# Two attentions: the spread of 1/sum by a transpose of reciprocals that ACT has written 64 times side by side

## The reference, cut to what matters

```python
# layer 0, latent tokens
s_nb = jnp.einsum('bqhd,biwhd->bhqiw', q_r, k_b) * scale + bias
s_cx = jnp.einsum('bqhd,bshd->bhqs', q_r, kc) * scale
p = jax.nn.softmax(jnp.concatenate([s_nb, s_cx], axis=-1), axis=-1)
o = einsum('bhqn,bnhd->bqhd', p[..., :n_nb], v_b) + einsum('bhqs,bshd->bqhd', p[..., n_nb:], vc)
# layer 1
s = jnp.einsum('bqhgd,bshd->bhgqs', q_b, k_all) * scale
p = jax.nn.softmax(s, axis=-1)
o = jnp.einsum('bhgqs,bshd->bqhgd', p, v_all)
```

## Time and profile before

| | |
|---|---|
| runs (3), us | 1558.33, 1562.14, 1561.76, median 1561.76 |
| the profiled execution, us | 1563.42, its span 1562.1 |
| PE busy | 1534.3 us, 98% of the span |
| PE weight loads | 1293.1 us, 83% |
| DVE busy | 928.9 us, 59% |
| ACT busy | 693.3 us, 44% |
| POOL busy | 64.7 us, 4% |
| DMA | 251 MB, mean 161 GB/s |
| attention 0, attention 1 | about 179 to 262 us and 755 to 809 us of the span |

### The profile page before, as it was taken

The page is one execution under the profiler, slowest core; times in us unless marked ns, Lnnn a source line. Parts: engine busy times, 40 slices in busy tenths (PEclk is TensorE's granted clock), DMA queues, the critical chain, the costliest instruction groups (busy, mean ns, idle before and its releaser), DMA issues.

```text
span 1562.1 us, 22713 instructions
## 1 busy us (share of the span) xinstructions
PE 1534.3 (98%) x9647; PEld 1293.1 (83%) x9647; DVE 928.9 (59%) x1208; ACT 693.3 (44%) x950; POOL 64.7 (4%) x92
## 2 busy tenths in 40 slices
PE   6999999999999999999999999999999999999998
PEld 4777766768888888879778888899999999999987
DVE  5422586463434333466866676668788856678863
ACT  4311475242312222235764545545555546555543
POOL 2010030000000000000000000034000000000000
PEclk9999999999999999999999999999999999999999
DMA  9664432654432332463134555665555554555552
GB/s 359 226 208 163 141 44 77 231 189 135 163 106 81 108 108 68 139 231 130 55 136 135 181 181 174 218 198 179 172 190 189 173 191 149 185 187 182 189 189 81
DMA packets 244165, 251.45 MB, mean 161 GB/s; under 512 B 17134, under 2 KB 237649, under 8 KB 244065
## 3 DMA queue, kind: packets, MB, share of 16 engines
q1 hardware_dynamic: 242528, 247.48, 48.8%
q0 software_dynamic: 928, 1.87, 0.3%
q10 hardware_dynamic: 608, 0.66, 0.1%
HBM read 248.94 MB, written 1.05 MB: 160 GB/s over the span
## 4 chain that ended last, share of the span: by engine, by line
PE 83%; DVE 7%; ACT 4%; POOL 2%; issue 2%; SPq 1%; DMA 1%; DVEq 0%; ACTq 0%; POOLq 0%
PE psum L366 80%; DVE wl L352 3%; ACT wh L345 3%; PE psum L954 2%; DMA raw<-in_na_w_qkv 1%; POOL ptmp L1860 1%; SPq L292 1%; DVE sums L1010 0%; DVE scr L1754 0%; ACT scr L1721 0%; DVE scr L1752 0%; DVE scr L1746 0%; POOL ptmp L1859 0%; DVE scr L542 0%; POOL scr L1867 0%
## 5 line engine op out<-in xcount | busy, mean ns | idle before, releaser
L352 DVE TENSOR_TENSOR wl<-raw,wh 128x2048 fp32r<-128x2048 f32 (+1 forms) x185 | 418.2, 2262 | 267.9 <-ACT wh L345 267.6
L345 ACT ACTIVATE wh<-raw 128x2048 fp32r<-128x2048 f32 (+1 forms) x185 | 348.0, 1883 | 380.2 <-PE psum L366 370.2
L366 PE MATMUL psum<-x,wh 128*128 128x256 f32 (+1 forms) x1792 | 446.0, 329 | 1.3 <-DVE x L552 0.8
L366 PE MATMUL psum<-x,wl 128*128 128x256 f32 x1248 | 351.6, 282 | 0.0
L366 PEld LDWEIGHTS psum<-x,wh 128*128 128x128 f32 x1792 | 302.3, 190 | 34.1 <-issue 3.1
L366 PE MATMUL psum<-xh,wh 128*128 128x512 f32 (+1 forms) x688 | 259.9, 378 | 3.1 <-DVE xl L705 2.4
L366 PE MATMUL psum<-xh,wl 128*128 128x512 f32 (+1 forms) x688 | 255.9, 372 | 0.0
L366 PE MATMUL psum<-xl,wh 128*128 128x512 f32 (+1 forms) x688 | 255.8, 372 | 0.0
L366 PEld LDWEIGHTS psum<-x,wl 128*128 128x128 f32 x1248 | 237.4, 190 | 0.1
L366 PEld LDWEIGHTS psum<-xh,wh 128*128 128x128 f32 x688 | 130.8, 190 | 35.3 <-issue 5.3
L366 PEld LDWEIGHTS psum<-xh,wl 128*128 128x128 f32 x688 | 130.7, 190 | 22.4
(11 more groups left out here) (277 smaller groups left out, 1957.0 us busy)
## 6 DMA issues: line engine op xcount, KB each, us to landing
raw<-in_ffn_w_in SPq DMA_DIRECT2D x44, 1024.0 KB, 5.0
pre<-in_ada_w SPq DMA_DIRECT2D x25, 1024.0 KB, 10.6
raw<-in_ada_w SPq DMA_DIRECT2D x23, 1024.0 KB, 5.5
raw<-in_w_ffn_gate SPq DMA_DIRECT2D x22, 1024.0 KB, 5.1
raw<-in_w_ffn_up SPq DMA_DIRECT2D x22, 1024.0 KB, 5.1
raw<-in_w_ffn_down SPq DMA_DIRECT2D x19, 1024.0 KB, 4.9
raw<-in_ffn_w_out SPq DMA_DIRECT2D x16, 1024.0 KB, 5.2
raw<-in_na_w_qkv SPq DMA_DIRECT2D x12, 1024.0 KB, 5.2
```

The lines of the kernel that those rows point to most:

```text
L345: act.e.activation(wh[:, c % NSPL, 0:z], raw[:, p % NRAW, 0:z], ACT.Copy).then_inc(W.hi, 1)
L352: dve.e.tensor_tensor(wl[:, c % NSPL, 0:z], raw[:, p % NRAW, 0:z], wh[:, c % NSPL, 0:z].bitcast(F32), ALU.subtract).then_inc(W.lo, 1)
L366: return pe.e.matmul(o, l, r, start=start, stop=stop, skip_group_check=shared)
```

## The change

A new tile `wide` (two groups, two query tiles, two heads, 64; 2 KiB a partition) takes the reciprocals, each written 64 times by ACT. For each group PE turns it with two transposes of 128x128, one for each query tile, both heads side by side. The reciprocals on DVE move ahead of the wait for the transposes and of DVE's copy. On ACT the wait for the reciprocals and the wide write stand after the exponentials and ahead of the copy L990. PE's wait for the reciprocals goes, since the wait for ACT's copy holds for the wide write too; that wait and DVE's stand ahead of the spread now. The tile's places in the arena and the tables' first column are the rest.

```diff
     def __init__(...)
+        self.wide = wide
...
+        wide0 = at(54, "wide0", [P, 2, 2, 2, 64])
+        wide1 = at(38, "wide1", [P, 2, 2, 2, 64])
...
             def values_part(g, first, last):
 
-                at_, u, nc_ = A_.groups[g]
+                u, nc_ = A_.groups[g]
                 o = bank[6 + g % 2]
                 if first:
-                    pe.wait_ge(S.recip, b_.recip + u + 1)
                     if g == 0 and value:
                         value()
                     if g >= 2:
                         pe.wait_ge(S.scaled, b_.scaled + g - 1)
-                    for x in range(2):
-                        for h in range(2):
-                            mm(o[64 * h:64 * h + 64, T + x * P:T + x * P + P], A_.sums[:, 2, at_ + x, h:h + 1].to_broadcast([P, 64]),
-                               ident, True, True)
                     pe.wait_ge(S.copied_a, b_.copied_a + u + 1)
                     pe.wait_ge(S.copied_d, b_.copied_d + u + 1)
+                    for x in range(2):
+                        pe.e.transpose(o[:, T + x * P:T + x * P + P], A_.wide[:, g % 2, x, :, :].rearrange("p h d -> p (h d)"), ident)
...
                 j = i - 2
                 if 0 <= j < n:
-                    g = A_.units[j][0]
-                    act.wait_ge(S.turned, b_.turned + j + 1)
+                    g, parts, x, at_ = A_.units[j]
                     if g >= 2:
                         act.wait_ge(S.pv, b_.pv + g - 1)
+                    act.wait_ge(S.recip, b_.recip + j + 1)
+                    act.e.activation(A_.wide[:, g % 2, x:x + parts, :, :],
+                                     A_.sums[:, 2, at_:at_ + parts, :].unsqueeze(3).to_broadcast([P, parts, 2, 64]), ACT.Copy)
+                    act.wait_ge(S.turned, b_.turned + j + 1)
                     to, o = turned(A_, j, 0)
                     act.e.activation(to, o, ACT.Copy).then_inc(S.copied_a, 1)
...
                 if 0 <= j < n:
                     g, parts, _, at_ = A_.units[j]
+                    dve.wait_ge(S.exp, b_.exp + 2 * j + 2)
+                    dve.e.reciprocal(A_.sums[:, 2, at_:at_ + parts, :], A_.sums[:, 1, at_:at_ + parts, :]).then_inc(S.recip, 1)
                     dve.wait_ge(S.turned, b_.turned + j + 1)
                     if g >= 2:
                         dve.wait_ge(S.pv, b_.pv + g - 1)
                     to, o = turned(A_, j, 1)
                     dve.e.tensor_copy(to, o).then_inc(S.copied_d, 1)
-                    dve.wait_ge(S.exp, b_.exp + 2 * j + 2)
-                    dve.e.reciprocal(A_.sums[:, 2, at_:at_ + parts, :], A_.sums[:, 1, at_:at_ + parts, :]).then_inc(S.recip, 1)
```

More of the change, by code:

```diff
@@ L83, with __init__ @@
 class Attention:
-    def __init__(self, S, base, units, groups, steps, pt, rb, sums, scale, rms, hi, lo):
+    def __init__(self, S, base, units, groups, steps, pt, rb, wide, sums, scale, rms, hi, lo):
         self.S, self.base, self.units, self.groups, self.steps = S, base, units, groups, steps
-        self.pt, self.rb, self.sums, self.scale, self.rms, self.hi, self.lo = pt, rb, sums, scale, rms, hi, lo
+        self.pt, self.rb, self.wide, self.sums, self.scale, self.rms, self.hi, self.lo = pt, rb, wide, sums, scale, rms, hi, lo
         self.n = len(units)
@@ L141, in program @@
         cz = rstd[:, :].rearrange("p (k n) -> p k n", k=KT)
-        pt0, rb0 = at(70, "pt0", [P, 2, 2, 4, T]), at(86, "rb0", [P, 2, T])
+        pt0, rb0, wide0 = at(70, "pt0", [P, 2, 2, 4, T]), at(86, "rb0", [P, 2, T]), at(54, "wide0", [P, 2, 2, 2, 64])
         xh1, xl1 = at(0, "xh1", [P, KT, TT], F32R), at(16, "xl1", [P, KT, TT], F32R)
@@ L151, in program @@
         xh4, xl4 = at(48, "xh4", [P, KT, T], F32R), at(56, "xl4", [P, KT, T], F32R)
-        pt1 = at(64, "pt1", [P, 2, 2, 4, T])
+        pt1, wide1 = at(64, "pt1", [P, 2, 2, 4, T]), at(38, "wide1", [P, 2, 2, 2, 64])
         acc2 = at(74, "acc2", [P, TT])
@@ L1049, in program @@
         units0 = [(2 * p + (kind > 0), 2 if kind == 0 else 1, max(kind - 1, 0), 4 * p + (0, 2, 3)[kind]) for p in range(8) for kind in range(3)]
-        groups0_ = [(4 * p + 2 * lat, 3 * p + 2 * lat, 4 if lat else 2) for p in range(8) for lat in range(2)]
+        groups0_ = [(3 * p + 2 * lat, 4 if lat else 2) for p in range(8) for lat in range(2)]
         steps0 = Steps(*zip(*[((3 * p + 5, 3 * p + 6, True, 3 * p + 6) if lat else (3 * p + 4, 3 * p + 4, False, 3 * p + 4))
@@ L1055, in side0 @@
             return slice(0, T) if g % 2 else slice(T, TT)
-        C0 = Attention(A0, A0._make([0] * len(A0)), units0, groups0_, steps0, pt0, rb0, sums0, lambda j, h: 1.0, None,
+        C0 = Attention(A0, A0._make([0] * len(A0)), units0, groups0_, steps0, pt0, rb0, wide0, sums0, lambda j, h: 1.0, None,
                        lambda g: xh1[:, g // 2, side0(g)], lambda g: xl1[:, g // 2, side0(g)])
@@ L1507, in program @@
         steps1 = Steps([2 * g + 4 for g in range(8)], [2 * g + 5 for g in range(8)], [False] * 8, [2 * g + 5 for g in range(8)])
-        C1 = Attention(A1, base1, [(j // 2, 1, j % 2, j) for j in range(16)], [(2 * g, 2 * g + 1, 4) for g in range(8)], steps1, pt1, rb1,
+        C1 = Attention(A1, base1, [(j // 2, 1, j % 2, j) for j in range(16)], [(2 * g + 1, 4) for g in range(8)], steps1, pt1, rb1, wide1,
                        sums0, lambda j, h: rms1(j)[:, h:h + 1], rms1, lambda g: xh4[:, g, :], lambda g: xl4[:, g, :])
```

## The result

| | before | after |
|---|---|---|
| first set of runs, median, us | 1560.39 (13 runs) | 1563.52 (13 runs) |
| ratio, 95% interval | | 1.0024 (1.0016 to 1.0033) |
| the same two kernels again, us | 1559.76 (17) | 1564.80 (6) |
| ratio, 95% interval | | 1.0033 (1.0022 to 1.0045) |
| profiled execution, us; span | 1563.42; 1562.1 | 1562.95; 1561.6 |

What follows compares the result with a forecast made beforehand. PE bounded both attentions before; after the change a round of ACT and DVE would. Attention 0 +4.9 and attention 1 +1.5 sum to +6.4 us: 1569.8 against the profiled 1563.42, 1568.2 as a median; range 1560.5 to 1573.5.

Steps and rivals of the forecast that it cites:

- The write's price: ACT's wide write of the repeated reciprocals: 0.20 us for 128 elements a partition, 0.31 us for 256.
- a dearer price: The Trainium skill's ACTIVATE price for ACT's wide writes, 0.41 and 0.51 us; it would have made the total +9.9 us.
- rb and handover to L1034: First unit with bias, attention 0: ACT writes rb in 0.41 us, then 0.10 us until DVE starts L1034.
- pair, attention 0: One ACT and DVE round over three units takes 10.9 us, against 9.70 for PE and 10.16 before.
- lead used up by the tenth score: Start of attention 0: the first pairs still have a lead to use up, +0.25 us by the tenth score.
- four full periods: Steady part of attention 0: four pairs, each 0.74 us longer than before, together +3.0 us.
- last pair and draining, attention 0: End of attention 0: the last pair's own period and about 1 us of late transposes, together +1.7 us.
- A handover costs 0.10 us: Between ACT and DVE in each unit: one engine starts 0.10 us after the other ends, read from two places.
- the walk: PE, ACT and DVE queues carried forward through both attentions, each instruction starting when queue and waits allow; total +6.4 us.
- The forecast's lower end, +3.7: Both attentions: wide writes of 0.15 us give +4.7, handovers of 0.05 us from DVE to ACT take another 1 off.
- rival E: TensorE's clock falls to half throughout both attentions, 67 us more, 1628 us in all; chance 0.02.
- A: The forecast itself: the round of ACT and DVE bounds both attentions, 1568.2 us, own range 1565.5 to 1571.7; chance 0.80.

## Why the prediction was right or wrong

**Right, step by step.** That PE alone bounded both stages; that the change takes some 5.5 us from it (with the reciprocals early, pairs of 9.73 and 6.08, forecast 9.70 and 6.07); that this does not arrive, because ACT's wait for a reciprocal that stands behind the maxima joins ACT and DVE into one round; which waits would show and about how long (0.61 to 1.23 us before the wide writes for 0.7 to 1.4, 0.55 to 0.82 on DVE for 0.7 to 0.9, 0.22 and 0.28 on PE for 0.3 to 0.4); that the round outlasts PE's pair. The write's price was right too: 0.21 us from start to start for 128 elements (228.94 to 229.15) and 0.32 for 256 (236.23 to 236.55), forecast 0.20 and 0.31. The prediction set the rows against a dearer price, 0.41 and 0.51 us, and that price was not the one for this write: the Trainium skill (ScalarE: Activation LUTs, Rules for kernel authors) gives it for an ACTIVATE whose bias is a pointer operand, and the wide write has none. For one with immediate scale and bias the same page of the Trainium skill (What ACT_TABLE_LOAD costs) has 186 ns and 0.833 ns an element, less some 93 ns where one overlaps the next. That makes an estimate of 0.29 and 0.40 us of duration, 0.20 and 0.31 from start to start, and the trace agrees: 0.31 and 0.42 of duration, 0.21 and 0.32 of step. What counts in the queue is the step.

**Wrong: the size,** 6.4 us forecast, 3.7 and 5.1 measured, 4.8 in the profile. The terms that were mis-sized:

| term | forecast | measured |
|---|---|---|
| reciprocal and handover to the write | 0.26 | 0.25, 0.19 (232.41 to 232.60) and 0.26 |
| rb and handover to L1034 | 0.41 + 0.10 | 0.41 (233.29 to 233.70) |
| unit without bias | 3.02 | 2.99 (227.49 to 230.48) |
| first unit with bias | 3.74 | 3.56 (230.48 to 234.04) |
| second unit with bias | 4.15 | 4.18 (234.04 to 238.22) |
| pair, attention 0 | 10.90 | 10.73 |
| maxima with L1015, attention 1 | 1.50 | 1.46 (788.63 to 790.09) |
| pair, attention 1 | 6.58 | 6.35 |
| lead used up by the tenth score | +0.25 | -0.1 |
| four full periods | +3.0 | +2.2 |
| last pair and draining, attention 0 | +1.7 | +1.7 |
| attention 0 | +4.9 | +3.8 |
| attention 1 | +1.5 | +1.0 |

The step that failed is "A handover costs 0.10 us", put on every link of the round alike. It was read from two rows, L1015 to ACT and xh to L1038, and it holds for xh to L1038 (230.04 to 230.14) and, at 0.09, for two reciprocals of three. From the other reciprocal to the write it is 0.04 (232.56 to 232.60), and from rb to L1034 0.03 (233.67 to 233.70); rb itself took 0.38 where 0.41 was put in. These two links, 0.19 for 0.26 and 0.41 for 0.51, make the whole difference in the pair of attention 0, 0.17 us, of which 0.03 is rb's own length. It is 1.6% of the round, but the forecast is made of a difference: 10.90 - 10.16 is 0.74, 10.73 - 10.16 is 0.57. In attention 1 the excess over PE's old pair was 0.05 instead of 0.28 us. The same two links account for 0.15 of these 0.23 us, and the maxima with L1015, 1.46 for 1.50 in each of two units, for the rest:

```profile
788.63 1.28 DVE L1010 TENSOR_REDUCE sums<-psum 128x1 f32<-128x512 f32 x2
...
790.09 0.16 DVE L1020 RECIPROCAL sums<-sums 128x2 f32<-128x2 f32 x1
...
790.28 0.31 ACT L986 ACTIVATE wide<-sums 128x128 f32<-128x128 f32 x1 [0.51 <-DVE sums L1020]
```

In attention 0 the links explain the four full periods (+2.2 for +3.0). Two parts of the gap stay open. The lead at the start of attention 0 was worth 0.35 us more than the walk gave it, and no run takes that apart. And the attentions together are 4.8 us longer in the profile, while the runs of the first set say 3.7 (2.5 to 5.1): what the rest of the program gives back in the median, no experiment separates.

The forecast's lower end, +3.7, is not this explanation, and that the first set of runs meets it is luck. It took writes of 0.15 us, which measured 0.21, and shortened only the handovers from DVE to ACT; the handover from ACT's rb to DVE, the larger part of the error in attention 0, it left at 0.10.

The range, 1560.5 to 1573.5, held the time; that "slower by over 0.3%" was given 0.68 is borne out by one set of runs (1.0033) and not by the other (1.0024); both intervals hold 1.003.

## What to carry to other kernels

A wait on the result of another engine is dear or free by what stands ahead of the producer in that engine's queue, not by how long the producer takes: look where the operand is made, and make it as soon as its own inputs allow (here one move in DVE's queue turned +3.7 to +5.1 us into -4.7). When an engine gets a new wait, write down the whole round through both queues, start to start, and compare it with the bound's period; busy shares of 86% and 72% gave no warning. And when a forecast is a small difference of two such periods, its error is that of the links, so give each link its own row.

## What the runs showed of the hardware that was not expected

Stretches at half clock stand or are missing at the same place of the program from one execution to the next. In the kernel before a PE gap of 0.91 us ends at 1033.3 us. The 15 us around it:

```profile
1030.00:1045.00 15.00, 14.09 (x101) 13.43 (x100) 10.21 (x15) 7.49 (x10) 3.66 (x7) 0.89 0.78 261
```

and the same 15 us of the kernel after, where a gap of 0.91 us ends at 1034.9:

```profile
1030.00:1045.00 15.00, 14.09 (x113) 13.44 (x112) 11.23 (x17) 8.71 (x12) 4.64 (x7) 1.00 0.76 250
```

101 matmuls against 113. The part of the program around this place (from the last residual of the first block's layer 1 to the closing transposes) takes 467.2 us in four of the ten profiles and 465.0 to 465.7 in six; the projections ahead of attention 1 take 68.8 or 68.9 us in four and 67.3 or 67.4 in six, and the change touches neither. The clock goes with it: the four long projections show 0.97 from 690 to 750 us, the six short ones 1.00. The times of single runs go with the clock too: of the first 13 of the kernel after, the six with a mean clock of 0.998 took 1562.0 to 1563.5 us, the four with 0.995 took 1564.3 to 1565.8. The second profile of the kernel after has such a stretch inside attention 0, where PE had waited 1.53 us for a copy:

```profile
260.00:264.00 4.00, 2.46 (x16) 2.16 (x14) 1.96 (x7) 2.78 (x10) 0.00 (x0) 0.81 0.00 0
264.00:268.00 4.00, 4.00 (x28) 2.03 (x26) 2.26 (x5) 2.00 (x5) 0.00 (x0) 0.77 0.01 4
```

In the first profile the same wait (1.53 us) was followed by a full clock. That is rival E in small: about 1.3 us, once, sometimes, where A at half clock throughout had been priced at 67. A steady part shows it once, in the run with the reciprocal behind the copy, whose PE gaps are up to 1.45 us:

```profile
225.00:228.00 3.00, 2.83 (x14) 2.31 (x16) 2.44 (x5) 2.24 (x10) 1.94 (x3) 0.55 0.03 9
...
231.00:234.00 3.00, 3.00 (x26) 1.78 (x26) 1.93 (x4) 0.97 (x3) 0.00 (x0) 1.00 0.22 26
```

There 14 matmuls were begun in 3 us, after a gap of 0.88 us, and 26 six us later. In the kernel after, with gaps of some 0.3 us, the steady parts of both profiles are at full clock, with ten transposes in place of eight and four products. The Trainium skill (TensorE: Matmul & The Clock Gate, Part 4: PE-mode transpose) has transposes not count as work for the clock; these two profiles show no fall in the steady parts that the added ones brought. What decides whether a gap is followed by half clock was not tried. These stretches are worth 1.3 to 2.2 us each, as much as the changes studied here, and one profiled span against another is therefore no measure of them: only cut into stages, or many runs, are.
